# Input projections of a two-layer hybrid decoder: the RMS factor applied before or after the product

## The reference

```python
def rmsnorm(x, g):
    y = x * lax.rsqrt(jnp.mean(x * x, axis=-1, keepdims=True) + EPS)
    return y * g
for l in range(DEPTH):
    h = rmsnorm(x, norm_mix[l])
    x = x + mixer(h, ...)      # u = h @ w_in, split into 13 parts; three head groups; @ w_out
    h = rmsnorm(x, norm_ffn[l])
    x = x + (swiglu(h, ...) if l % 2 == 0 else moe_ffn(h, ...))
return rmsnorm(x, norm_final)
```

## Time and profile before

| | |
|---|---|
| median of 3 runs | 1423.79 us (1423.51 to 1425.75) |
| the profiled execution | 1421.93 us; its span 1420.1 us |
| busy share of the span | PE 94%, PEld 58%, DVE 67%, ACT 48%, POOL 10% |
| granted PE clock over the span | 0.991 |
| chain that ended last | PE 73%, DVE 16%, ACT 7%, issue 2%, DMA 2% |
| HBM | 218 MB read, 177 GB/s over the span |

### The profile page before, as it was taken

The page is one execution under the profiler, slowest core; times in us unless marked ns, Lnnn a source line. Parts: engine busy times, 40 slices in busy tenths (PEclk is TensorE's granted clock), DMA queues, the critical chain, the costliest instruction groups (busy, mean ns, idle before and its releaser), DMA issues.

```text
span 1420.1 us, 25135 instructions
## 1 busy us (share of the span) xinstructions
PE 1332.8 (94%) x10417; PEld 819.1 (58%) x10417; DVE 955.8 (67%) x1549; ACT 687.2 (48%) x1037; POOL 143.7 (10%) x117
## 2 busy tenths in 40 slices
PE   5999899999999999999999999989999999999992
PEld 2346445434444444444346444559978988978971
DVE  6875897465540254215875787667788788888886
ACT  4435776234220223102345775346476676676672
POOL 0010410320000000031010200440400000000003
PEclk9999999999999999999999999999999999999996
DMA  5531585315420244002521100238899899989975
GB/s 198 193 102 30 192 295 187 134 48 200 153 90 0 113 153 162 0 0 80 198 90 31 30 1 8 68 126 337 326 380 369 313 350 376 346 341 364 337 285 193
DMA packets 39992, 255.59 MB, mean 180 GB/s; under 512 B 5626, under 2 KB 6650, under 8 KB 25418
## 3 DMA queue, kind: packets, MB, share of 16 engines
q1 hardware_dynamic: 30346, 220.14, 41.7%
q0 software_dynamic: 8960, 33.26, 7.1%
q10 hardware_dynamic: 576, 0.64, 0.1%
HBM read 218.28 MB, written 33.65 MB: 177 GB/s over the span
## 4 chain that ended last, share of the span: by engine, by line
PE 73%; DVE 16%; ACT 7%; issue 2%; DMA 2%; POOL 0%; ACTq 0%; DVEq 0%; SPq 0%
PE bank L1101 18%; PE bank L1103 18%; PE bank L1102 17%; DVE arena L911 6%; ACT arena L769 4%; PE bank L1304 3%; PE bank L1350 2%; PE bank L1320 2%; DVE bank L2030 2%; DVE arena L2053 1%; PE bank L1211 1%; PE bank L1148 1%; PE bank L1210 1%; PE bank L1198 1%; DVE arena L1738 1%
## 5 line engine op out<-in xcount | busy, mean ns | idle before, releaser
L911 DVE SCALAR_TENSOR_TENSOR arena<-arena 128x3072 f16<-128x3072 f32 x86 | 288.8, 3358 | 57.1 <-ACT arena L769 56.5
L769 ACT ACTIVATE arena<-arena 128x3072 f16<-128x3072 f32 x86 | 237.0, 2756 | 0.0
L1101 PE MATMUL bank<-arena 128*128 128x144 bf16 (+3 forms) x880 | 214.2, 263 | 10.0 <-DVE arena L911 5.1
L1103 PE MATMUL bank<-arena 128*128 128x144 bf16 (+3 forms) x880 | 214.0, 262 | 0.0
L1102 PE MATMUL bank<-arena 128*128 128x144 f16 (+3 forms) x880 | 214.0, 262 | 0.0
L1101 PE MATMUL bank<-hh,wring_hi 128*128 128x512 bf16 x352 | 133.8, 380 | 1.5 <-DVE hl L1752 1.5
L1101 PE MATMUL bank<-hh,arena 128*128 128x512 bf16 x352 | 133.6, 380 | 1.2 <-DVE hl L1752 0.9
L1103 PE MATMUL bank<-hh,wring_lo 128*128 128x512 bf16 x352 | 133.6, 379 | 0.0
L1102 PE MATMUL bank<-hl,arena 128*128 128x512 f16 x352 | 133.5, 379 | 0.0
L1103 PE MATMUL bank<-hh,arena 128*128 128x512 bf16 x352 | 133.5, 379 | 0.0
L1102 PE MATMUL bank<-hl,wring_hi 128*128 128x512 f16 x352 | 133.5, 379 | 0.0
(11 more groups left out here) (327 smaller groups left out, 2651.6 us busy)
## 6 DMA issues: line engine op xcount, KB each, us to landing
arena<-in_ew SPq DMA_DIRECT2D x86, 1536.0 KB, 8.7
arena<-in_dw SPq DMA_DIRECT2D x22, 1536.0 KB, 6.7
wstage<-in_w_chunk SPq DMA_DIRECT2D x44, 512.0 KB, 3.6
expert_results<-iota POOLq DMA_DIRECT2D x9, 2048.0 KB, 21.2
arena<-in_cmp_w SPq DMA_DIRECT2D x2, 2048.0 KB, 9.0
expert_slots<-iota POOLq DMA_DIRECT2D x5, 512.0 KB, 18.9
expert_results<-wstage SPq DMA_DIRECT2D x5, 512.0 KB
arena<-in_w_tok SPq DMA_DIRECT2D x2, 1096.0 KB, 6.2
```

The costliest lines, as they stand in the source:

```text
L769: act.activation(ew_hi_[:, G % EP, :], ew[:, G % ES, :], ACT.Copy, scale=SW).then_inc(M["hi_ready"], 1)
L911: dve.scalar_tensor_tensor(out=ew_lo_[:, G % EP, :], in0=ew[:, G % ES, :], scalar=SW, in1=ew_hi_[:, G % EP, :], op0=ALU.mult, op1=ALU.subt ...
L1101: pe.matmul(out, w_hi, x_hi, start=first, stop=False)
L1103: return pe.matmul(out, w_lo, x_hi, start=False, stop=last)
```

## The change

The input of the projections becomes `xT` times the gain, without the factor, for both layers. The factor (`mix_rstd`, the same on every partition) multiplies each of the feature results as DVE takes it out of PSUM; for the token results four small matmuls turn it into one number per row, which ACT applies as its scale. The norm's sum moves behind the first two feature chunks. The last dense down results are split as they arrive. Loads are reordered: `pp` (all small parameters, norm weights among them) goes first on SP's queue instead of third on ACT's, and the first two weight chunks stand between the loads of x. PREPARE is reordered, mostly by moving latent and rope steps one or two chunks later. POOL splits no token blocks: DVE makes four remainders, ACT four `tok_h` straight from the staged rows. The first expert weight part is rounded before the first gathered copy. The gains times 16 are computed once at the start for all three uses. Not shown: waits renamed to match, one dictionary entry per new step, and PE's wait for the last dense result, which moves behind the first two chunks.

```diff
@@ -80,18 +80,18 @@
...
-    ("feat", 0), ("feat", 1), ("squares", "q"),
-    ("feat", 2), ("norm", "q"), ("squares", "kv"),
-    ("feat", 3), ("norm", "kv"), ("rope", ("kpe", 0)),
-    ("feat", 4), ("conv", 0), ("uq", 0), ("uq", 1),
-    ("feat", 5), ("conv", 1), ("uq", 2), ("uq", 3),
-    ("feat", 6), ("rope", ("kc", 0)), ("uq", 4), ("uq", 5),
-    ("feat", 7), ("uk", 0), ("rope", ("ks", 0)),
-    ("feat", 8), ("win", 0), ("uk", 1),
+    ("feat", 0), ("feat", 1), ("rms", 0),
+    ("feat", 2), ("squares", "q"),
+    ("feat", 3), ("norm", "q"), ("squares", "kv"),
+    ("feat", 4), ("norm", "kv"), ("rope", ("kpe", 0)), ("conv", 0),
+    ("feat", 5), ("conv", 1), ("uq", 0), ("uq", 1),
+    ("feat", 6), ("rope", ("kc", 0)), ("uq", 2), ("uq", 3),
+    ("feat", 7), ("uk", 0), ("uq", 4), ("uq", 5),
+    ("feat", 8), ("win", 0), ("rope", ("ks", 0)), ("uk", 1),
     ("feat", 9), ("rope", ("kw", 0)), ("wtok", 0), ("uk", 2), ("lam", 0),
     ("feat", 10), ("hid", 0), ("rope", ("q", 0)), ("lru_gates", 0), ("lru_gates", 1),
@@ -357,7 +357,9 @@
...
-        gain_sx = small[:, 244:252]
+        gains = sb("gains", 3 * KC)
+        gain_mix, gain_sx = [gains[:, l * KC:(l + 1) * KC] for l in range(2)], gains[:, 2 * KC:3 * KC]
+        mix_rstd = hf[:, 1, :]
@@ -817,11 +816,12 @@
...
+            first_hi(0)
             for j in range(KC):
                 gathered(0, j, bank[GATHER_BANK[j % 4]], 0, CAPS[0])
-                if j in (2, 4):
-                    first_hi(j // 2 - 1)
-            for p in (2, 3, 4):
+                if j in (3, 5):
+                    first_hi(j // 2)
+            for p in (3, 4):
                 first_hi(p)
@@ -945,7 +945,7 @@
...
-            for i in range(TT - TOK_POOL):
+            for i in range(TT):
                 token_lower(dve, i)
@@ -1109,24 +1108,35 @@
...
-                place[0] = 1
-                if l == 0:
...
+                place[0] = 0
+                def mix_sum(_):
+                    if l == 0:
+                        b = take(("ssq", l, "mix"), ("rms", l, "mix"))
+                        pe.wait_ge(*ready("summed", KC - 1))
+                        pe.matmul(b[:, :], ones[:, :], early, start=True, stop=True
+                                  ).then_inc(*signal("ssq", l, "mix", 0))
+                    else:
+                        norm_sum_late((l, "mix"))
+                def tok_scale(_):
+                    b = take(("tok", l, "scale"), ("tok", l, "scale"))
+                    pe.wait_ge(*ready("rstd", l, "mix"))
+                    for i in range(TT):
+                        mm = pe.matmul(b[:, i:i + 1], mix_rstd[:, i * P:(i + 1) * P], ident[:, 0:1], start=True, stop=True)
+                    mm.then_inc(*signal("tok_mm", l, "scale"))
                 def first_feats():
                     pair = [take(("feat", l, j), ("feat", l, j)) for j in range(2)]
                     if l == 0:
-                        spare(pe, 6, pair[0], ones[:, :], early)
+                        for _ in range(12):
+                            pe.matmul(pair[0][:, 0:P], ones[:, :], ones[:, :], start=True, stop=True)
                     for j in range(2):
                         pe.wait_ge(*ready("w_lo", NW * l + j))
-                    if l > 0:
-                        spare(pe, 26, pair[0], wring_hi[:, NW * l % WR, 0, :], wring_hi[:, NW * l % WR, 0:4, :])
                     for k in range(KC):
+                        pe.wait_ge(*ready("hh", l, "mix", k))
                         pe.wait_ge(*ready("hl", l, "mix", k))
                         for j in range(2):
                             name, c, rows, p0 = FEAT[j]
...
+                    if l > 0:
+                        pe.wait_ge(D["y_added"], KC * (HALVES + 1))
@@ -1452,47 +1464,52 @@
...
-            for name, dst in (("eps", eps), ("ones", ones), ("pp", pp)):
+            for name, dst in (("ones", ones), ("eps", eps)):
                 act.dma_start(dst[:, :], io[name]).then_inc(*signal("first_consts", by=16))
...
-                if l > 0:
-                    for J in range(NW * l, NW * l + WS):
-                        w_hi(J)
+                def mix_hi(k):
+                    act.activation(hh[:, k, :], xT[:, k, :], ACT.Copy,
+                                   scale=gain_mix[l][:, k:k + 1]).then_inc(*signal("hh", l, "mix", k))
                 act.activation(rms[:, 0:1], eps[:, 0:1], ACT.Sqrt)
                 if l == 0:
+                    act.wait_ge(*ready("staged", "gain"))
                     for k in range(KC):
                         if k % 2 == 0:
                             act.wait_ge(*ready(f"x_loaded{k // 2}"))
+                        mix_hi(k)
+                        if k in (1, 3):
+                            w_hi(k // 2)
+                    w_hi(WS)
+                    for k in range(KC):
                         if k >= SQ0:
                             act.wait_ge(*ready("summed", max(k - SQ0, 1)))
                         act.activation(first_sq(k), xT[:, k, :], ACT.Square).then_inc(*signal("sq", l, "mix", k))
-                    for J in range(WS):
+                else:
+                    for J in range(NW * l, NW * l + WS):
                         w_hi(J)
-                else:
+                    for k in range(KC):
+                        if k == KC - 2:
+                            w_hi(NW * l + WS)
+                        act.wait_ge(D["y_added"], KC * HALVES + k + 1)
+                        mix_hi(k)
                     squares((l, "mix"), [(xT[:, KC - 1, :], P, x_ready(l, 0))])
-                root((l, "mix"), 1, DM)
-                halves((l, "mix"))
...
                 def feat(j):
-                    name, c, rows, p0 = FEAT[j]
-                    act.wait_ge(*ready("w_used", NW * l + j))
-                    b = bank[ring_of[("feat", l, j)]]
-                    if (name, c) == ("qdn", 1):
-                        rows = Q_RANK - P
-                        act.activation(kpe[NOPE:DQK, :], b[NOPE:DQK, :], ACT.Copy,
-                                       scale=1.0 / (SW * SX)).then_inc(*signal("kpe_up", l))
-                    act.activation(home[name](c)[p0:p0 + rows, :], b[p0:p0 + rows, :],
-                                   ACT.Copy, scale=(SCALE_NSA if name == "q" else 1.0) / (SW * SX)
-                                   ).then_inc(*signal("feat", l, j))
                     if j < NF - 1:
                         w_hi(NW * l + j + WR)
+                def tok_scale(_):
+                    act.wait_ge(*ready("tok_mm", l, "scale"))
+                    act.activation(total, bank[ring_of[("tok", l, "scale")]][:, 0:TT], ACT.Copy,
+                                   scale=1.0 / (SW * SX)).then_inc(*signal("tok", l, "scale"))
+                    act.wait_ge(*ready("tok", l, "scale"))
...
-                                   scale=1.0 / (SW * SX)).then_inc(*signal("tok", l, i))
+                                   scale=total[:, i:i + 1]).then_inc(*signal("tok", l, i))
...
                     for i in range(TT):
-                        if i >= TT - TOK_POOL:
-                            act.wait_ge(*ready("tok_l_pool", "scaled", i))
-                            act.copy(tok_h[:, i, :], staged[:, i, :]).then_inc(*signal("tok_h", i))
-                            continue
                         act.activation(tok_h[:, i, :], staged[:, i, :], ACT.Copy,
                                        scale=total[:, i:i + 1]).then_inc(*signal("tok_h", i))
...
+                dve.wait_ge(*ready("hh", l, "mix", k))
+                dve.scalar_tensor_tensor(out=hl[:, k, :], in0=xT[:, k, :], scalar=gain_mix[l][:, k:k + 1],
+                                         in1=hh[:, k, :], op0=ALU.mult, op1=ALU.subtract
+                                         ).then_inc(*signal("hl", l, "mix", k))
...
-                    if not ahead and m >= KC - WS:
-                        w_remainder(NW + m - (KC - WS))
+                    if not ahead and KC - 1 - WR <= m < KC - 1:
+                        w_remainder(NW + m - (KC - 1 - WR))
...
+                    if not ahead:
+                        dve.wait_ge(D["y_added"], e * KC + KC + m + 1)
+                        mix_lower(1, m)
...
-            dve.wait_ge(*ready("first_consts"))
+            dve.wait_ge(*ready("pp_loaded"))
+            for a, (l, name) in enumerate(((0, "norm_mix"), (1, "norm_mix"), (1, "norm_ffn"))):
+                ins = dve.tensor_scalar(gains[:, a * KC:(a + 1) * KC], par(l, name, 0, KC), SX, None, ALU.mult)
+            ins.then_inc(*signal("staged", "gain"))
+            dve.wait_ge(*ready("staged", "gain"))
...
                 if l == 0:
+                    for k in range(KC):
+                        mix_lower(l, k)
+                        if k in (1, 3):
+                            w_remainder(k // 2)
+                    w_remainder(WS)
                     for k in range(1, KC):
                         dve.wait_ge(*ready("sq", l, "mix", k))
                         if k >= 2:
```

(49 more changed lines are left out.)

44 lines of the change are left out of this document (17 added, 27 removed).

## The result

| | before | changed |
|---|---|---|
| median of the runs, us | 1424.40 (4 runs, 1423.5 to 1425.8) | 1406.78 (4 runs, 1404.4 to 1411.0) |
| ratio to before | | 0.9877, 95% interval 0.9861 to 0.9893 |
| profiled execution, time and span, us | 1421.93, 1420.1 | 1406.31, 1404.3 |

The account below looks back on a forecast made before the run. PE, busy 94% of the span, was taken as the bound, so only its waits or spares could yield time. Terms -8.4 - 8.0 + 1.8 + 0.3 - 3.5 = -17.8 us took 1423.8 to 1406.0; range 1400 to 1416.

Parts of the forecast that it names:

- Layer 0's start: First projections of layer 0: PE starts at 13.7, chunk 2 at 27.0 in place of 35.45; -8.4 us.
- PE waits 1.9 us for it, adds 0.96: Layer 0 behind chunks 0 and 1: PE waits 1.9 us for the sum, then 0.96 for its matmul.
- Layer 1's start: From dense end to projections: PE goes on without a gap, chunk 2 at 662.9 in place of 670.87; -8.0 us.
- Token factor: Four float32 matmuls on PE ahead of token results, 0.9 us each time; +1.8 us for both layers.
- Evictions: Projection results move from ACT to DVE, nearly free with 1.4 us smallest slack at kc's rope; +0.3 us.
- every us of DVE beyond 1.4 is one of PE: Projections, at kc's rope: if the cover fails, DVE delay beyond 1.4 us of slack costs PE the same.
- Start of the MoE: Without POOL's work DVE's stretched instructions shorten: gather 4.4 us earlier, first SiLU at 957.6; -3.5 us.
- DVE as the bound: Rival, projections: DVE's evictions delay PE at kc's rope; 1433 us (slower, chance 0.05), milder form 1412 (0.15).
- POOL isn't what slows DVE: Rival, start of the MoE: DVE's slow instructions stay slow, MoE term 0; 1409.5 us, chance 0.12.
- Layer 0's data: Rival, layer 0's start: ones or the third weight chunk lands 3.5 us later; 1409.5 to 1411 us, chance 0.08.
- The stretched DVE instructions: MoE router chain: POOL taken as cause through a shared port lock; three instructions give back 4.4 us.

Follow-up runs that it names:

- gap_spares: Changed kernel, with 11 spare PE matmuls ahead of the wait for layer 0's sum; 1404.04 us, ratio to before 0.9861.
- l1_no_overlap: Changed kernel, but PE starts layer 1's projections only when the last slice of hl is there; 1409.61 us, ratio to before 0.9911.
- squares_first: Changed kernel, with layer 0's squares on ACT and additions on DVE ahead of the third weight chunk's split; 1402.37 us, ratio to before 0.9850.
- late_kc: Changed kernel, with one unread DVE reciprocal of 3.35 us ahead of chunk 5's (kc) eviction in each layer; 1412.43 us, ratio to before 0.9921.
- old_order: Changed kernel with PREPARE in the order of before, only the two new steps put in; 1417.60 us, ratio to before 0.9948.
- evict_twice: Changed kernel, but DVE does each eviction from chunk 2 on twice, first into an unread buffer; 1407.00 us, ratio to before 0.9882.
- after_pool: Changed kernel with GpSimd's two token blocks put back; 1407.84 us, ratio to before 0.9879.
- before_no_pool: Kernel before, with GpSimd splitting no tokens and DVE and ACT taking all four blocks; 1420.18 us, ratio to before 0.9971.
- rms_earlier: squares_first, with the sum's step in PREPARE also moved ahead of ('feat', 1); 1404.26 us, ratio to before 0.9864.
- after_again: The changed kernel run once more, unedited, as base of the first batch; 1405.35 us, ratio to before 0.9868.
- old_loads: Changed kernel, but pp is again the last load of ACT's queue, behind eps and ones; 1408.33 us, ratio to before 0.9884.

## Why the prediction was right, step by step

The forecast of 1406.0 stands beside 1406.8. The four places, their causes and their order of size were as said. That the total is this close is luck, as its terms were not: on the profiled execution 17.8 was forecast and 15.6 measured (the base, below).

- **Layer 0's start**, -8.4 forecast, -6.5 measured once chunk 2 runs at its own pace. PE's start (13.7 forecast, 13.15), the third chunk (18.2; rounded from 18.6) and the end of the sum (26.0; 26.3) were as worked out. Three readings on the way were not right and cost little: `pp` (53 KB) is not the smallest load of its queue, which is `eps` (0.5 KB); the 16.59 of the earlier trace rows is the length of POOL's idle time, and the constant landed by 17.04, when its row starts; and loads don't take at least 5.1 us, as `pp` landed 2.0 and `ones` 2.2 us after their issue in the changed kernel. ACT started at 6.88 even so (7.3 forecast), because `eps` took 5.7. What failed is "PE waits 1.9 us for it, adds 0.96": the wait was put in at its own length only. Behind the 2.69 us of idle time the clock was at half, and the sum took 1.34 and six matmuls 0.43 each, 1.7 us more. gap_spares and l1_no_overlap show the size. As to the cause: of the seven traces with this wait five have the fall at its end or behind it (from 26.2 to 27.2 us on), of the four in which it was filled or gone none. So the wait brings the fall in most executions, not in all. The remedy that was not seen is that the sum needn't be late at all (squares_first).
- **Layer 1's start**, -8.0 forecast, -8.2 measured, with PE going on without a gap as said.
- **Token factor**, +1.8 forecast for both layers, 0.8 us each measured.
- **Evictions**, +0.3 forecast; +0.2 is seen between token result 0 and the last dense result in layer 0, +0.1 between token result 0 and the last residual in layer 1. Slack at kc 1.4 forecast, 1.2 measured; late_kc shows that place and price were right for one long delay, and old_order that the late steps of PREPARE are the cover. The sentence "every us of DVE beyond 1.4 is one of PE" holds only for work that DVE can't put into idle time of its own: evict_twice added 2.4 us up to kc and moved it by 0.6.
- **Start of the MoE**, -3.5 forecast, -3.7 measured; gather 4.4 earlier forecast, 5.4 measured. The difference is two more stretched instructions (L2150 and L2153 of before, the 0.55 and 0.83 in the rows of after_pool) that the sum left out; the wait for the splits (2.0) was exact. Both kernels with one setting of the split turned over give 3.5 as well.
- **After it**, nothing was forecast, and 0.9 us is lost between the first SiLU and the end of the span; a microsecond of the kind described under what stays open is in it.
- **The rivals.** DVE as the bound didn't come in this kernel, and comes with 3.35 us more. "POOL isn't what slows DVE" is excluded by before_no_pool and after_pool. Layer 0's data were as late as the likeliest case had them.
- **The stretched DVE instructions.** The trace of after_pool shows L2229 held to within 0.03 us of the end of GpSimd's TENSOR_TENSOR (929.51 + 2.12), and L2213 with its plain 0.19 inside GpSimd's TENSOR_SCALAR. L2205 lasted 1.22 in place of 0.42 and ended at 925.23, within the first of the two TENSOR_SCALARs, which lasted from 923.83 to 926.70. The Trainium skill (SBUF — State Buffer, § Who interferes with whom) has the shared port pair locked for a whole instruction: the first row agrees; the other two don't, and show that overlap alone doesn't hold a DVE instruction, and that one that is held need not be held to the end of GpSimd's. How a TENSOR_SCALAR of GpSimd holds DVE stays open.

The base of the prediction should also be named: the profiled execution of before lay 2.5 us under its median, that of the changed kernel 0.5 under its own, and so a sum that was 2.2 too large against the traces fits the medians. The interval of the ratio (15 to 20 us) holds both 15.6 and 17.8, so the runs don't say which of the two is nearer; the stages do.

## What to carry to other kernels

A factor that is common to a whole contraction can be moved from its operands to its results when the results' engine has slack at the first consumer, and that slack is found by walking one engine's list against the other's, not from busy shares: here a DVE that was busy for 9.56 of 10 us took the evictions for nothing, and 3.35 us at one place cost PE 2. A new wait of PE like the ones here (2.0 to 2.7 us) is to be priced twice, at its length alone and with the matmuls behind it at half clock, as both happened. It can be filled with spares, or better removed by asking what stands ahead of the late work in its queue. Work given to an idle GpSimd beside a chain of small DVE instructions can cost the chain more than it saves.

## What the runs showed of the hardware

- The same wait of PE was followed by the lower clock in some traces and not in others. Ahead of layer 0's sum (2.66 to 2.75 us) five of seven fell, and old_order and l1_no_overlap didn't. Of late_kc's two waits, 2.05 us in layer 0 had no fall and 2.06 in layer 1 had one. The wait of 2.0 us ahead of the gather's second half had one in three traces of eleven (evict_twice, rms_earlier, l1_no_overlap). In the kernel before and in after_pool a wait of 2.28 us in the router's chain had one, and the longer one of 2.95 us ahead of the gather had none. The same code pays or doesn't, and the length of a wait alone doesn't tell which.
- Short stretches at half clock also turn up around attention in some executions of a kernel and not in others (late_kc at 128.6, evict_twice at 156.1 and 784.2, none there in after_again). With them goes the spread of the times: the five runs of after_again took 1402.8, 1403.5, 1405.4, 1405.5 and 1410.5 us at mean granted clocks of 0.993, 0.992, 0.991, 0.991 and 0.988.
- A DVE instruction beside GpSimd was stretched to nearly the same length in both traces that had the overlap (L2170 1.98 and its like 1.99, L2174 2.21 and 2.21).
- Open: the last SiLU comes 14.7 us after the one three before it in five traces (the changed kernel, after_again, squares_first, gap_spares, old_loads) and 13.7 in the other nine, with and without GpSimd's blocks (evict_twice, old_order and late_kc as well as the kernel before and after_pool). In the changed kernel ACT starts it 1.2 us after PE ends the group that it reads, not 0.2 as in after_pool. Since changed kernels stand on both sides, it can't be put down to the change; no run was made for its cause.
